# Two-layer block kernel on one core: the second mixer's merge in high and low parts

## The reference

```python
gates = jax.nn.sigmoid((gl + b_gate[l]).astype(jnp.float32)).astype(x.dtype)
gates = gates.reshape(B, S, N_BRANCH_2, D)
merged = (gates[:, :, 0] * (o_fox @ w_fox_o[l])
          + gates[:, :, 1] * (o_swa @ w_swa_o[l])
          + gates[:, :, 2] * (o_mem @ w_mem_o[l]))
x = x + merged @ w_out[l]
```

## Time and profile before

| | |
|---|---|
| median of three runs | 4846.75 us (4840.98 to 4851.11) |
| the profiled execution | 4835.18 us, its span 4833.4 us |
| mean granted clock of PE | 0.886 of full speed |
| PE busy | 3646.0 us (75%), DVE 2797.6 us (58%), ACT 1103.9 us (23%), POOL 1151.9 us (24%) |
| matmuls of line 1221 in this merge | 64.0 us (two branches) and 30.2 us (the third) over both halves |
| matmuls of the gather, lines 232 and 233 | 1146.3 us and 1085.8 us |

### The profile page before, as it was taken

One profiled execution on the slowest core, in us unless ns is written; L12 is line 12 of the kernel. 1 busy time (PEld: TensorE's weight loads), 2 busy tenths in 40 slices (PEclk: granted clock), 3 DMA queues, 4 the chain that ended last, 5 costly groups with the idle time before them and its releaser, 6 DMA issues. The chain is left out here.

```text
span 4833.4 us, 41734 instructions
## 1 busy us (share of the span) xinstructions
PE 3646.0 (75%) x13654; PEld 2152.9 (45%) x13654; DVE 2797.6 (58%) x6402; ACT 1103.9 (23%) x2607; POOL 1151.9 (24%) x1028
## 2 busy tenths in 40 slices
PE   4946699784767677788688686697868876677777
PEld 3834698463333232553366452452346653222222
DVE  5557755436844677555554457754555557755554
ACT  1104000121122122224432221232533221111111
POOL 0000000001423354222222123232222223343332
PEclk9978777887989999898899898798989999899999
DMA  4500000222978899787688687686669877899998
GB/s 176 185 27 3 4 1 5 68 69 111 408 310 345 348 414 408 296 314 270 246 315 316 246 310 308 233 325 224 244 237 338 303 294 308 341 373 420 414 420 361
DMA packets 202356, 1248.85 MB, mean 258 GB/s; under 512 B 24796, under 2 KB 29276, under 8 KB 67428
## 3 DMA queue, kind: packets, MB, share of 16 engines
q0 software_dynamic: 147456, 1073.81, 56.6%
q1 hardware_dynamic: 54184, 172.51, 10.7%
q10 hardware_dynamic: 512, 0.03, 0.0%
HBM read 1241.76 MB, written 4.46 MB: 258 GB/s over the span
## 5 line engine op out<-in xcount | busy, mean ns | idle before, releaser
L215 POOL DMA_INDIRECT held_pair<-in_experts,held_expert x1024 | 1151.7, 1125 | 3651.2 <-PE held_acc L233 2445.8
L277 DVE CUSTOM_DVE_ANT_0 held_pair<-held_pair,held_hrow 128x1024 f32<-128x1024 f32 x1024 | 1246.3, 1222 | 540.2 <-DMA held_pair<-in_experts,held_expert 494.0
L232 PE MATMUL held_acc<-held_pair,held_diag 128*128 128x512 f32 x2048 | 1146.3, 642 | 387.6 <-ACT held_diag L257 327.6
L233 PE MATMUL held_acc<-held_pair,held_diag 128*128 128x512 f32 x2048 | 1085.8, 613 | 0.0
L232 PEld LDWEIGHTS held_acc<-held_pair,held_diag 128*128 128x128 f32 x2048 | 351.3, 197 | 895.7 <-ACT held_diag L257 670.9
L257 ACT ACTIVATE held_diag<-held_ident,held_weight 128x128 f32<-128x128 f32 x1024 | 402.4, 394 | 1266.6 <-DVE held_weight L272 1233.9
L233 PEld LDWEIGHTS held_acc<-held_pair,held_diag 128*128 128x128 f32 x2048 | 404.2, 197 | 520.8 <-issue 520.8
L250 ACT ACTIVATE held_bent<-held_dot 128x2 f32<-128x2 f32 x512 | 102.8, 201 | 540.7 <-DVE held_dot L277 502.1
L500 PE MATMUL pgh_ps<-pgh_hhi,pgh_whi 128*128 128x256 f32 x384 | 127.4, 332 | 28.9 <-DVE pgh_wlo L519 28.9
L500 PE MATMUL p2h_ps<-p2h_hhi,p2h_whi 128*128 128x256 f32 x368 | 123.4, 335 | 31.0 <-DVE p2h_wlo L519 31.0
L1284 PE MATMUL c_ps<-c_keys,held_room 128*128 128x128 f32 x256 | 45.3, 359 | 131.0 <-DMA c_iota<-in_iota 131.0
(11 more groups left out here) (516 smaller groups left out, 5509.1 us busy)
## 6 DMA issues: line engine op xcount, KB each, us to landing
pgh_raw<-in_w_in SPq DMA_DIRECT2D x48, 512.0 KB, 6.7
p2h_raw<-in_w_in SPq DMA_DIRECT2D x46, 512.0 KB
p_raw<-in_w_in SPq DMA_DIRECT2D x34, 512.0 KB, 3.5
p_w_ada<-in_w_ada SPq DMA_DIRECT2D x16, 1024.0 KB, 6.3
held_pair<-in_experts,held_expert POOLq DMA_INDIRECT x1024
e2qh_raw<-in_w_peer_q SPq DMA_DIRECT2D x32, 512.0 KB, 8.0
ada_w<-in_w_ada SPq DMA_DIRECT2D x4, 2048.0 KB, 11.3
e1q_raw<-in_w_query SPq DMA_DIRECT2D x16, 512.0 KB, 3.7
```

What stands on the lines that cost most here:

```text
L215: pool.indirect_dma_start(self.pair[m % BUFS][:], None, self.layers[t // TT][0], bass.IndirectOffsetOnAxis(ap=self.expert[:, t % TT, s:s + ...
L232: pe.matmul(self.acc[0][:], diag[:], up[:, 0:512], start=s == 0, stop=s == NJ - 1)
L233: pe.matmul(self.acc[1][:], diag[:], up[:, 512:D], start=s == 0, stop=s == NJ - 1).then_inc(self.added, 1)
L277: ins = dve.tensor_tensor_reduce(down, down, self.hrow[:, t % TT, :], 1.0, 0.0, ALU.mult, ALU.add, self.dot[:, t % 2, s:s + 1])
```

## The change

The second mixer calls a new function instead of `merge_stage` (the first mixer keeps the old one). In the new one

- ACT copies the three branches' values into float32r tiles `ohi` (12 copies of 128x256) and the weights of each product into `whi` (two tiles in turn, 128x512); DVE makes `olo` and `wlo` by subtraction;
- a product is 12 matmuls in place of 4: for each inner chunk `whi` by `ohi`, `whi` by `olo`, `wlo` by `ohi`;
- the weights land in one ring of three tiles `raw`, and a tile is loaded again when the low part has been made from it;
- ACT's list begins with values of branch 0, weights 0, values of branches 1 and 2, weights 1, then the 24 gates; the weights of product n+2 come at point n, ahead of the gather's pieces, and wait for product n;
- DVE's list has the low part of weights n+2 behind the multiplication of product n.

```diff
@@ second_mixer @@
-    merge_stage(nc, own("mg2"), gates, 0, [(ins["w_fox_o"], foxT), (ins["w_swa_o"], swaT), (ins["w_mem_o"], memT)], h,
-                bias=cols("b_gate_2"), tokens=HALF, beats=beats["mg"])
+    merge_by_parts_stage(nc, own("mg2"), gates, [(ins["w_fox_o"], foxT), (ins["w_swa_o"], swaT), (ins["w_mem_o"], memT)], h, 4,
+                         cols("b_gate_2"), HALF, beats["mg"])
@@ new: merge_by_parts_stage @@
+        ohi, olo = r.sb("ohi", [P, nb, kc, tokens], F32R), r.sb("olo", [P, nb, kc, tokens], F32R)
+        raw = [r.sb(f"raw{u}", [P, kc, P]) for u in range(3)]
+        whi, wlo = [[r.sb(f"{n}{u}", [P, kc, P], F32R) for u in range(2)] for n in ("whi", "wlo")]
...
+            def _(sp):
+                for n in range(N):
+                    if n >= 3:
+                        sp.wait_ge(w_lo, n - 2)
+                    sp.dma_start(raw[n % 3][:], branches[n % nb][0][n // nb]).then_inc(w_ready[n % 3], 16)
...
+            def _(act):
+                def high_of_values(i):
+                    for c in range(kc):
+                        act.activation(ohi[:, i, c, :], branches[i][1][:, c, :], ACT.Copy).then_inc(o_hi, 1)
+
+                def high_of_weights(n):
+                    act.wait_ge(w_ready[n % 3], 16 * (n // 3) + 16)
+                    if n >= 2:
+                        act.wait_ge(made, n - 1)
+                    act.activation(whi[n % 2][:], raw[n % 3][:], ACT.Copy).then_inc(w_hi, 1)
+
+                high_of_values(0)
+                high_of_weights(0)
+                for i in range(1, nb):
+                    high_of_values(i)
+                high_of_weights(1)
+                for m in range(DC):
+                    for i in range(nb):
+                        gate = gates[:, i * DC + m, :]
+                        act.activation(gate, gate, ACT.Sigmoid, bias=bias[:, i * DC + m:i * DC + m + 1]).then_inc(squashed, 1)
+                for n in range(N):
+                    if n + 2 < N:
+                        high_of_weights(n + 2)
+                    beats.act(act, n)
...
+            def _(pe):
+                for n in range(N):
+                    i = n % nb
+                    pe.wait_ge(o_lo, kc * min(n + 1, nb))
+                    pe.wait_ge(w_lo, n + 1)
+                    if n >= 5:
+                        pe.wait_ge(taken, n - 4)
+                    got = ps[n % 5][:, 0:tokens]
+                    for c in range(kc):
+                        hi, lo = whi[n % 2][:, c, :], wlo[n % 2][:, c, :]
+                        pe.matmul(got, hi, ohi[:, i, c, :], start=c == 0, stop=False)
+                        pe.matmul(got, hi, olo[:, i, c, :], start=False, stop=False)
+                        last = pe.matmul(got, lo, ohi[:, i, c, :], start=False, stop=c == kc - 1)
+                    last.then_inc(made, 1)
+                    beats.pe(pe, n)
...
+            def _(dve):
...
+                def low_of_weights(n):
+                    dve.wait_ge(w_hi, n + 1)
+                    dve.tensor_tensor(wlo[n % 2][:], raw[n % 3][:], whi[n % 2][:].bitcast(F32), ALU.subtract).then_inc(w_lo, 1)
...
+                low_of_values(0)
+                low_of_weights(0)
+                for i in range(1, nb):
+                    low_of_values(i)
+                low_of_weights(1)
+                for m in range(DC):
+                    for i in range(nb):
+                        n = nb * m + i
+                        dve.wait_ge(squashed, n + 1)
+                        dve.wait_ge(made, n + 1)
+                        dve.tensor_tensor(part[:, i, :], ps[n % 5][:, 0:tokens], gates[:, i * DC + m, :], ALU.mult).then_inc(taken, 1)
+                        if n + 2 < N:
+                            low_of_weights(n + 2)
+                        if i == nb - 1:
+                            dve.wait_ge(taken, n + 1)
+                        beats.dve(dve, n)
```

More of the change, by code:

```diff
@@ L1239, in _, with merge_by_parts_stage, low_of_values @@
                         link(dve.tensor_tensor(out[:, m, :] if last else part[:, 0, :], part[:, 0, :], part[:, i, :], ALU.add))
+def merge_by_parts_stage(nc, name, gates, branches, out, kc, bias, tokens, beats):
+    nb = len(branches)
+    N = nb * DC
+    beats = beats.over(N)
+    with ExitStack() as stack:
+        r = Room(nc, stack, name)
+        ohi, olo = r.sb("ohi", [P, nb, kc, tokens], F32R), r.sb("olo", [P, nb, kc, tokens], F32R)
+        raw = [r.sb(f"raw{u}", [P, kc, P]) for u in range(3)]
+        whi, wlo = [[r.sb(f"{n}{u}", [P, kc, P], F32R) for u in range(2)] for n in ("whi", "wlo")]
+        part = r.sb("part", [P, nb, tokens])
+        ps = [r.ps(f"ps{u}") for u in range(5)]
+        made, taken, squashed, o_hi, o_lo, w_hi, w_lo, chain = r.sem("made", "taken", "squashed", "o_hi", "o_lo", "w_hi", "w_lo", "chain")
+        w_ready = [r.sem(f"w_ready{u}") for u in range(3)]
+        with nc.Block() as block:
+            @block.gpsimd
+            def _(pool):
+                beats.pool(pool)
+            @block.sync
+            def _(sp):
[3 more added lines that the diff above has]
+                    sp.dma_start(raw[n % 3][:], branches[n % nb][0][n // nb]).then_inc(w_ready[n % 3], 16)
+            @block.scalar
+            def _(act):
[20 more added lines that the diff above has]
+                    beats.act(act, n)
+            @block.tensor
+            def _(pe):
[13 more added lines that the diff above has]
+                    beats.pe(pe, n)
+            @block.vector
+            def _(dve):
+                link = Chain(dve, chain)
+                def low_of_values(i):
+                    for c in range(kc):
+                        dve.wait_ge(o_hi, kc * i + c + 1)
+                        dve.tensor_tensor(olo[:, i, c, :], branches[i][1][:, c, :], ohi[:, i, c, :].bitcast(F32), ALU.subtract).then_inc(o_lo, 1)
+                def low_of_weights(n):
[17 more added lines that the diff above has]
+                        beats.dve(dve, n)
+                    for i in range(1, nb):
+                        last = i == nb - 1
+                        link(dve.tensor_tensor(out[:, m, :] if last else part[:, 0, :], part[:, 0, :], part[:, i, :], ALU.add))
```

## The result

The changed kernel took 4859.54 us in the median of 13 runs, the kernel before 4843.29 us in 13 runs beside them. The ratio is 1.0030, with a 95% interval from 1.0021 to 1.0039: 14.5 us slower (10.2 to 18.9). The two medians are 16.2 us apart, which lies in that interval. The difference is small, but the interval does not reach down to no change.

The account below looks back on a forecast made before the run. ACT was taken to bound each merge's start and PE the rest; per half +7.7 (later start) + 2.4 (half clock) - 6.1 (faster products) = +4.0 us, for both +8.0, on 4846.75 giving 4855 us, range 4847 to 4868.

Parts of the forecast that it names:

- The likeliest case: Whole kernel: difference within 0.2%, or 9.7 us, so not to be told from no change; chance 0.52.
- PE bounds the steady part, and a product saves 0.29 us: The 67.3 us after each merge's start: PE always busy; 21 products at 1.43 instead of 1.73 us save 6.1 us.
- ACT's list sets the start: Merge start: weights 2 copied behind all 24 sigmoids, product 2 at 18.9 us, its following slot 7.7 us later than before.
- Half clock, 2.6 us: After some 6 us idle at each merge's start, PE returns at half clock, losing 2.6 us, 0.2 inside a wait.
- Start in all, 10.1 us: Start of each merge: 7.7 us of later slot plus 2.4 us of clock loss, 10.1 us per half.
- Steady additions at nothing; DVE has room: Steady part: ACT's 20 copies and DVE's 20 subtractions hide behind PE, cost nothing; DVE 49.5 us busy in about 61.
- The ring should just hold: Three weight tiles in the steady part: lead 6.4 to 8.1 us against landing of 4.8 median, 7.8 at most.
- the rival on late weights: Steady part: late weights delay ACT's copy and DVE's list, PE waits, products lose their 0.29 us; 4867 us; chance 0.25.
- Sum: Both merges: each half +7.7 + 2.4 - 6.1 = +4.0 us, for both +8.0 us.
- the clock did not stay up: Rival at merge start: 6 us idle ends before PE's clock falls, each half costs 1.6 us; 4850 us; chance 0.12.
- the start was not given back: Rival: later stretches or product 2 regain the whole start, leaving the 12.2 us gain; 4834.5 us; chance 0.05.
- The draining: Rival at the start's table load: ACT's queue must empty behind copies, 1.38 us more per half; 4857.5 us; chance 0.05.

## Why the prediction was right, and where not

The forecast was 4855 us, 8.0 us slower, in a range of 4847 to 4868; 4859.54 us lies in it. Part of that is luck. The change itself is 14.5 us, nearly twice the forecast and above the +4 to +12 us that the forecast gave itself. The absolute time came closer because the 8 us were added to 4846.75 us, the median of three, while the kernel before took 4843.29 us beside the changed one. The likeliest case, no change that can be told, did not come: the interval begins at 10.2 us, beyond the 9.7 named as the bound. The mechanism of the start was right. By its own sign ("if it waits for subtractions or transfers in the later part") the forecast was wrong for the steady part. Step by step, in the first half:

- *PE bounds the steady part, and a product saves 0.29 us*: right. 3.14 us for product and slot in place of 3.45.
- *ACT's list sets the start*: right, and shown by putting it alone into the old kernel and by taking it away. Product 2 at 18.6 us (forecast 18.9), its slot at 21.3 (forecast 20.5, before the loss by the clock).
- *Half clock, 2.6 us*: 2.2 us by the kernel in which PE was kept at work.
- *Start in all, 10.1 us*: 8.5 us to the slot and 1.0 behind it, 9.5 us.
- *Steady additions at nothing; DVE has room*: right. DVE was busy 47.5 of 62.2 us, the subtraction 0.69 us, the copy 0.63.
- *The ring should just hold*: this is the term that was mis-sized. I compared the lead of 6.4 to 8.1 us with a median landing of 4.8 us and gave late weights "some 2 us" in the range and nothing in the sum. That median was a weak base: it mixes the steady part with the start of the stage, and the trace of the kernel before has landings for only 16 of the 48 transfers. In its steady parts alone (2600 to 2665 and 3750 to 3816 us) they have a median of 5.7 and 4.9 us. In the changed kernel's steady parts it is 6.6 and 7.1 us, and 8.6 at most, beyond the lead. PE lost 2.3 us by them in the first half and 2.1 in the second, and with the ring of four this went. The prediction let the diagonals stand behind ACT's copy with a product to spare. The trace shows the longer chain: DVE's subtraction waits for the late copy, and the small product that the diagonal needs stands behind the subtraction. That PE would wait through DVE's list is what the rival on late weights had said.
- *Sum*: to the last slot 9.5 - 6.3 (21 products at 0.30) + 2.3 = +5.5 us against the forecast +4.0; measured +5.5 and +5.7, and +5.9 and +5.7 for the whole merges.

The two merges account for 11.6 of the 14.5 us. The remaining 3 us lie inside the interval and were found in no stage.

Of the rivals, the late weights came true for a third of their price (2.3 of 6.1 us in a half); the clock did not stay up; the start was not given back, since the whole kernel is slower. The draining was not seen: 1.28 us from the load to the first sigmoid, with copies in front of it. Where the Trainium skill (ScalarE: Activation LUTs, section "What ACT_TABLE_LOAD costs") counts 1380 ns of draining for each switch, this trace has none that adds to the time.

## What to carry to other kernels

A faster product on the busiest engine is worth only what its preparation does not cost on the engine that gates the stage's start: write down when each engine's first needed result comes, not only the steady rates. Put preparation where an engine idles anyway (here DVE at the start), and count what else stands behind a new wait in an in-order list, on every engine that the wait passes through. When a stage gets faster, its transfers' lead in time shrinks with it, so a ring may have to grow. Size it by the landing times of the stretch that it serves, and by the long ones among them, not by a median over the whole stage.

## What the runs showed of the hardware

- A float32 matmul of 256 columns took 0.43 us from start to start, the three float32r ones in its place 0.36 us (1.43 us for twelve). With 512 columns, in the first mixer's merge, it was 0.86 us against 0.68 us (18 of the new matmuls took 4.09 us, and three of them replace one). The three-part product gains 17% and 21%, at full clock.
- PE was back at half clock after 6.72 us of idleness. With useless matmuls in that gap it worked on at full clock, and product 3 started 2.2 us earlier.
- Behind shorter waits the clock fell in some merges only: 1.91 to 2.74 us of waiting in four merges, with 1.5 us lost at half clock in the slot behind it or the product after that; 1.72 to 1.83 us in four others, with nothing lost.
- Landing in the second mixer's merge took 4.8 us in the median (7.6 at most) in one kernel with the ring of three and 5.9 us (8.6 at most) in another: the same transfers hold PE up in one and not in the other.
